# Stage changes of a fused transformer kernel run by token halves

## The reference, cut to what matters

```python
# first block; gate(i), shift(i), scale(i) come from silu(c) @ w_ada + b_ada
h = h + 0.5*gate(0)*rmsnorm(swiglu(modulate(rmsnorm(h, g_pre[0]), shift(0), scale(0))), g_post[0])   # ffn0
p = modulate(rmsnorm(h, g_pre[1]), shift(1), scale(1)) @ w_in      # in_v, in_i, in_t
o = concat([rmsnorm(sparse_attention(p)), rmsnorm(stick_breaking_attention(p))]) @ w_out             # out
h = h + gate(1)*rmsnorm(o, g_post[1])
h = h + 0.5*gate(2)*rmsnorm(swiglu(modulate(rmsnorm(h, g_pre[2]), shift(2), scale(2))), g_post[2])   # ffn1
# second block
h = h + diff_attention(rms_norm(h, attn_norm_g[0])) @ w_o          # v, qk, o_a
h = h + sq_relu_mlp(rms_norm(h, mlp_norm_g[0]))                    # mlp0
h = h + mla_attention(rms_norm(h, attn_norm_g[1]), latents of rms_norm(h, kv_in_norm_g)) @ w_o       # dkv, dq, ..., o_b
h = h + sq_relu_mlp(rms_norm(h, mlp_norm_g[1]))                    # mlp1
return rms_norm(h, final_norm_g)
```

## Time and profile before

| | us |
|---|---|
| median of 3 runs | 1226.72 (1226.50 to 1229.63) |
| the profiled execution | 1227.54 |
| its span, first to last instruction | 1226.2 |
| TensorE busy | 1171.4 (96%) |
| VectorE busy | 796.8 (65%) |
| ScalarE busy | 618.6 (50%) |
| GpSimd busy | 55.8 (5%) |
| mean granted TensorE clock | 0.985 of full speed |

### The profile page before, as it was taken

How to read it: one execution, slowest core, us unless ns; L and a number is a source line. 1 busy time by engine, 2 the same in 40 slices (tenths; PEclk the granted TensorE clock), 3 DMA queues, 4 the chain that set the end, 5 groups by cost and what they waited for, 6 DMA issues and landing times.

```text
span 1226.2 us, 19544 instructions
## 1 busy us (share of the span) xinstructions
PE 1171.4 (96%) x7742; PEld 1074.6 (88%) x7742; DVE 796.8 (65%) x1310; ACT 618.6 (50%) x1114; POOL 55.8 (5%) x75
## 2 busy tenths in 40 slices
PE   4999999999988999999999899999999889999998
PEld 4988799899977999999989788999998778899997
DVE  4879788758654666565667776555557665655554
ACT  5644343646654644444545455554546545555453
POOL 3100000000000000000002110000000100000000
PEclk9999899999998999999999989999999999999999
DMA  8969999443222365654343223545454414554540
GB/s 348 401 261 415 352 344 348 154 180 138 104 98 75 124 240 207 224 218 172 138 176 138 83 104 127 200 175 197 181 190 151 175 35 154 175 200 176 194 150 35
DMA packets 34010, 231.78 MB, mean 189 GB/s; under 512 B 3704, under 2 KB 5120, under 8 KB 6528
## 3 DMA queue, kind: packets, MB, share of 16 engines
q1 hardware_dynamic: 31952, 226.24, 49.9%
q10 hardware_dynamic: 1968, 4.29, 1.0%
HBM read 229.45 MB, written 1.06 MB: 188 GB/s over the span
## 4 chain that ended last, share of the span: by engine, by line
PE 78%; DVE 11%; ACT 5%; issue 2%; DMA 2%; POOL 1%; ACTq 0%; DVEq 0%; SPq 0%; POOLq 0%
PE ps L392 35%; PE pacc L392 34%; DVE wlo L355 3%; PE ps L402 2%; PE ps L405 2%; ACT wk L1020 2%; PE pacc L402 2%; DVE raw L333 1%; DMA raw<-in_stream 1%; ACT whi L354 1%; POOL st L499 1%; PE ps L531 1%; PE pacc L531 1%; DVE st L1015 1%; DVE tmp L668 1%
## 5 line engine op out<-in xcount | busy, mean ns | idle before, releaser
L355 DVE TENSOR_TENSOR wlo<-raw,whi 128x1024 fp32r<-128x1024 f32 x353 | 430.6, 1226 | 194.8 <-ACT whi L354 188.0
L354 ACT ACTIVATE whi<-raw 128x1024 fp32r<-128x1024 f32 x353 | 368.4, 1054 | 164.8 <-PE pacc L392 84.2
L392 PE MATMUL ps<-nhi,whi 128*128 128x256 f32 x1272 | 368.3, 290 | 1.8 <-DVE arena L1270 1.0
L392 PE MATMUL ps<-nlo,whi 128*128 128x256 f32 x1272 | 361.9, 284 | 0.0
L392 PE MATMUL ps<-nhi,wlo 128*128 128x256 f32 x1272 | 361.7, 284 | 0.0
L392 PEld LDWEIGHTS ps<-nhi,whi 128*128 128x128 f32 x1272 | 245.9, 193 | 7.3 <-DVE arena L1270 1.3
L392 PEld LDWEIGHTS ps<-nlo,whi 128*128 128x128 f32 x1272 | 245.9, 193 | 4.9 <-issue 0.8
L392 PEld LDWEIGHTS ps<-nhi,wlo 128*128 128x128 f32 x1272 | 245.7, 193 | 0.0
L743 ACT ACTIVATE sg<-ps 128x256 f32<-128x256 f32 x104 | 39.8, 383 | 164.5 <-PE ps L392 164.3
L392 PE MATMUL pacc<-whi,mhi 128*128 128x512 f32 x240 | 96.5, 402 | 2.4 <-DVE mlo L1192 2.4
L392 PE MATMUL pacc<-wlo,mhi 128*128 128x512 f32 x240 | 94.5, 394 | 0.0
(11 more groups left out here) (305 smaller groups left out, 1784.8 us busy)
## 6 DMA issues: line engine op xcount, KB each, us to landing
raw<-in_stream SPq DMA_DIRECT2D x213, 1024.0 KB, 4.9
gates<-in_g_post ACTq DMA_DIRECT2D x3, 512.0 KB, 6.4
h<-in_x SPq DMA_DIRECT2D x1, 1024.0 KB, 7.0
cst<-in_const ACTq DMA_DIRECT2D x1, 1024.0 KB, 4.8
arena<-bias_rows ACTq DMA_DIRECT2D x1, 1024.0 KB, 18.8
out<-tmp SPq DMA_DIRECT2D x4, 256.0 KB, 2.1
silu_c<-in_c_row ACTq DMA_DIRECT2D x1, 512.0 KB, 5.9
arena<-in_final_g SPq DMA_DIRECT2D x1, 512.0 KB, 5.7
```

Source lines behind the costliest of these rows:

```text
L354: t_hi = act.do(lambda e: e.activation(whi[:, s, :], src, ACT.Copy), arrived, room)
L355: t_lo = dve.do(lambda e: e.tensor_tensor(wlo[:, s, :], src, whi[:, s, :].bitcast(F32), ALU.subtract), arrived, room, t_hi)
L392: return e.matmul(o, lt[a], rh[b], start=start and first, stop=stop and last)
```

## The change

- `last_two` becomes `last_units`: the last three units (`LAST = 3`) run for token half 0, then for half 1. Three hooks of a new class `Crossing` take the place of `residual` and `to_parts`: `first` once half 0 is summed, `between` ahead of half 1's last unit, `second` once half 1 is summed.
- With a gate, y times gate is multiplied before the root of y is known, and the root enters the update of h.
- Turning, scaling and splitting are done for each half by itself, in pairs of chunks: two ScalarE steps of 128 tokens, then one VectorE copy and one subtraction for both chunks. The pieces are interleaved in a written order, with `feed(limit=1)` among them. The second half's turn and parts stand in `finish`.
- The next stage's first four units of `in_v` and `v` run half by half (`lead=cross.finish`: half 0 of two units, `finish`, half 0 of two more, then half 1 of all four); `dkv` and `dq` do likewise. `mlp0`, `mlp1` and `ffn1` begin after `finish`.
- After `mlp1` (`Ending`), h times the final gain is formed before the root, and each half is written by itself.
- `stream_plan`: the eight `ada` units of modulation 7 move from `ffn0` to `in_v`; `IN_ORDER` is another.

```diff
-IN_ORDER = [8, 9, 10, 11] + [g + j for g, j in ((12, 0), (16, 0), (12, 1), (16, 1), (12, 2), (16, 2), (0, 0), (4, 0),
-                                                (12, 3), (16, 3), (0, 1), (4, 1), (0, 2), (4, 2), (0, 3), (4, 3))]
+IN_ORDER = [8, 9, 12, 16, 10, 11, 13, 17, 14, 18, 15, 19, 0, 4, 1, 5, 2, 6, 3, 7]
...
-            if n < j - 1:
+            if n < min(j - 1, blocks - LAST):
                 steps.append(("down", n))
...
-    plan += spread(ffn("ffn0_", DFF // P, ("gate", "up"), 8), (2, 3, 4, 5, 6, 7), 1.03)
-    plan += [("in_v", k) for k in range(8)] + [("in_i", 0)]
+    plan += spread(ffn("ffn0_", DFF // P, ("gate", "up"), 8), (2, 3, 4, 5, 6), 1.05)
+    plan += spread([("in_v", k) for k in range(8)] + [("in_i", 0)], (7,), 1.0)
     plan += [("in_t", j) for j in IN_ORDER]
     plan += [("out", k) for k in OUT_ORDER]
...
-        def feed(until=None):
-            while not hold and pos["unit"] < (until or len(plan)):
+        def feed(until=None, limit=100):
...
+        def last_units(names, meeting, cross, between=None):
+            units, meets, done = [], [], [[None, None], [None, None]]
+            for i in range(2):
+                for n, name in enumerate(names):
+                    if i == 0:
+                        units.append(Unit(name))
+                        meets.append(meeting(n))
+                    meet, late = meets[n]
+                    for f in range(2):
+                        done[i][f] = products([(fix[2 * i + f].ap, [(meet[i], units[n].part(f * 512, f * 512 + 512), late)],
+                                                False, n == len(names) - 1)], units[n].ready)
+                    if i:
+                        units[n].release(done[1][1])
+                        if n == len(names) - 2:
+                            cross.between()
+                    elif between is not None and n < len(names) - 1:
+                        between()
+                if i == 0:
+                    cross.first(done[0])
+            cross.second(done[1])
...
+            if lead is not None:
+                units, start = [], 4
+                for i in range(2):
+                    for n in range(start):
+                        if i == 0:
+                            units.append(Unit(names[n]))
+                        k = chunks[n]
+                        unit_half(n, units[n], i, parts.tokens(k, i), parts.half[k, i])
+                        if i:
+                            units[n].release(done[1][1])
+                            feed()
+                        elif n == 1:
+                            lead()
...
+        class Crossing:
+            def __init__(self, outs, slot=None, gate=None, table=None):
+                self.outs, self.slot, self.gate, self.table = outs, slot, gate, table
+                self.q, self.p, self.r, self.held, self.z = {}, {}, {}, {}, {}
+                self.done, self.diag, self.gated = {}, {}, {}
+            def squares(self, src, n, sums, *after):
+                junk, f = arena[:, 6144 + 512 * n:6656 + 512 * n], n % 2
+                return act.do(lambda e: e.activation(junk, src, ACT.Square, scale=D ** -0.5,
+                                                     accum_out=sums[:, f:f + 1]), *after)
+            def root(self, sums, *after):
+                v, r = new_stat(), new_stat()
+                t = dve.do(lambda e: e.scalar_tensor_tensor(v, sums[:, 0:1], EPS, sums[:, 1:2], ALU.add, ALU.add), *after)
+                return r, power(r, v, t)
+            def begin(self, i, f):
+                w, y, d = slice(f * 512, f * 512 + 512), fix[2 * i + f], self.done[i][f]
+                if f == 0:
+                    self.q[i] = new_stat(2)
+                t = self.squares(y.ap, 2 * i + f, self.q[i], d)
+                tg = dve.do(lambda e: e.tensor_tensor(tmp[:, i, w], y.ap, gates[:, self.slot, w], ALU.mult), t, self.gate())
+                y.free = [tg]
+                self.gated[i, f], self.summed = tg, t
+            def mean(self, i):
+                self.r[i] = self.root(self.q[i], self.summed)
+            def update(self, i, f):
+                w, y = slice(f * 512, f * 512 + 512), fix[2 * i + f]
+                if f == 0:
+                    self.p[i] = new_stat(2)
+                if self.slot is None:
+                    t = dve.do(lambda e: e.tensor_tensor(h[:, i, w], h[:, i, w], y.ap, ALU.add), self.done[i][f])
+                    y.free = [t]
+                else:
+                    r, t_r = self.r[i]
+                    t = dve.do(lambda e: e.scalar_tensor_tensor(h[:, i, w], tmp[:, i, w], r, h[:, i, w], ALU.mult,
+                                                                ALU.add), t_r, self.gated[i, f])
+                self.summed = self.squares(h[:, i, w], 4 + 2 * i + f, self.p[i], t)
+            def ends(self, i):
+                self.r[i] = self.root(self.p[i], self.summed)
+            def diagonal(self, i):
+                r, t = self.r[i]
+                self.diag[i] = diagonal(i, r, t)
+            def turn(self, i):
+                self.held[i] = []
+                for g in range(4):
+                    b = banks.take()
+                    for c in range(2):
+                        k = 2 * g + c
+                        tk = pe.do(lambda e: e.matmul(b.ap[:, c * P:(c + 1) * P], h[:, i, k * P:(k + 1) * P], dg[:, i, :],
+                                                      start=True, stop=True), self.diag[i], b.free)
+                    self.held[i].append((b, tk))
+                dg_free[i] = [tk]
+            def scaled(self, i, *pairs):
+                w = slice(i * P, i * P + P)
+                for g in pairs:
+                    b, tk = self.held[i][g]
+                    for n, (parts, scale, shift, after) in enumerate(self.outs):
+                        for c in range(2):
+                            k, o, z = 2 * g + c, b.ap[:, c * P:(c + 1) * P], self.zs(n)
+                            if shift is None:
+                                t = act.do(lambda e: e.activation(z[:, k, w], o, ACT.Copy, scale=scale(k)), tk, after())
+                            else:
+                                t = act.do(lambda e: e.activation(z[:, k, w], o, ACT.Identity, bias=shift(k),
+                                                                  scale=scale(k)), tk, after())
+                        self.z[n, i, g] = t
+                    banks.give(b, t)
+            def zs(self, n):
+                z = arena[:, 6144:8192] if n else wk[:, 0:6, :].rearrange("p a b -> p (a b)")[:, 0:8 * T]
+                return z.rearrange("p (c t) -> p c t", c=8)
+            def split(self, i, *pairs):
+                for g in pairs:
+                    for n, (parts, scale, shift, after) in enumerate(self.outs):
+                        z = self.zs(n)[:, 2 * g:2 * g + 2, i * P:i * P + P]
+                        hi, lo = (a[:, 2 * g:2 * g + 2, i * P:i * P + P] for a in (parts.hi, parts.lo))
+                        t1 = dve.do(lambda e: e.tensor_copy(hi, z), self.z[n, i, g])
+                        t2 = dve.do(lambda e: e.tensor_tensor(lo, z, hi.bitcast(F32), ALU.subtract), t1)
+                        for k in (2 * g, 2 * g + 1):
+                            parts.half[k, i] = [t1, t2]
+                            if i:
+                                parts.t[k] = parts.half[k, 0] + parts.half[k, 1]
+            def first(self, done):
+                self.done[0] = done
+                if self.slot is None:
+                    self.update(0, 0)
+                    self.update(0, 1)
+                    self.ends(0)
+                    self.diagonal(0)
+                    return
+                self.begin(0, 0)
+                self.begin(0, 1)
+                self.mean(0)
+                if self.table is not None:
+                    act.quiet(self.table)
+                self.update(0, 0)
+                self.update(0, 1)
+            def between(self):
+                if self.slot is None:
+                    self.turn(0)
+                    self.scaled(0, 0, 1)
+            def second(self, done):
+                self.done[1] = done
+                if self.slot is None:
+                    self.update(1, 0)
+                    self.split(0, 0)
+                    self.update(1, 1)
+                    self.scaled(0, 2, 3)
+                    self.split(0, 1)
+                    self.ends(1)
+                    self.split(0, 2)
+                    self.diagonal(1)
+                    self.split(0, 3)
+                    busy(8)
+                else:
+                    self.begin(1, 0)
+                    self.ends(0)
+                    self.begin(1, 1)
+                    self.diagonal(0)
+                    self.mean(1)
+                    busy(20)
+                    self.turn(0)
+                    self.scaled(0, 0, 1)
+                    self.split(0, 0)
+                    self.update(1, 0)
+                    self.update(1, 1)
```

(69 more changed lines are left out.)

235 lines of the change are left out of this document (79 added, 156 removed).

## The result

The changed kernel took 1246.55 us (median of 4 runs, 1245.26 to 1247.86) against 1226.61 for the kernel before beside it: a ratio of 1.0161, 95% interval 1.0135 to 1.0188. It is slower, as forecast, but by 20 us and not by 9.5, and half a microsecond outside the range. The profiled execution's span is 1246.4; the page's first part now reads

The account below looks back on a forecast made before the run. TensorE is busy 96% of the span, so time can only come from pauses, half-speed stretches and instructions without products. 23 + 2 - 0.5 - 1 - 5 - 9 = +9.5 on the median 1226.7 gives 1236 us, range 1219 to 1246.

Parts of the forecast that it names:

- the crossings: The six stage changes, with their waiting, turns and queueing, cost +23 in sum; bounds -2 and +28.
- The clock: PE falls to half speed after a pause, with those in `out` and `v` named: one drop, +2; bounds 0 and 12.
- Rival (3): PE's clock falls in every crossing, at the second turn, after pauses of 1.6 to 4 us: 1242 to 1246; chance 0.16.
- The queues: DVE and ACT issue order at the crossings delays half 1's diagonal and parts; counted within the crossings' +23.
- The lost cover: At `o_a` and `o_b`, half 0's turn no longer covers half 1's chain: +1.8 each if only this counts.
- The root beside the splits: At the crossings, GpSimd's root collides with VectorE splits on the shared SBUF interface: 0.4 at each.
- The plans: Moving modulation 7 out of `ffn0` gives -5; the new `IN_ORDER` gives -9 around `in_t` and `out`.
- The end: After `mlp1`, half 0 is written early and fewer, shorter DVE steps follow the last root: -0.5 (0 to -1).
- The -1 for the waits ahead of the last blocks: Four hidden layers wait 0.26 before their last block; three units now stand ahead: -1.

Follow-up runs that it names:

- fills: Changed kernel with more products of nothing: 44 for 20 ahead of `out`'s second turn, 20 ahead of the third chunk at `ffn1`, `mlp0`, `mlp1`; 1244.75 us.
- mend: Changed kernel without `finish`'s weight unit at `ffn1`, `mlp0`, `mlp1`, lambda load issued ahead of `ffn1`, 44 products of nothing ahead of `out`'s second turn; 1227.81 us.
- mend_turn: `mend` and `turn_behind` together: the three mends and the other order of the no-gate crossings; 1226.32 us (0.9994).
- turn_behind: Changed kernel with, at no-gate crossings, half 0's turn behind half 1's last product, half 1's chain ahead of splits, 4 products of nothing for 20; 1240.25 us.
- lead_turn: `lead_limit` with `turn_behind`'s order at `mlp0` and `mlp1` and no weight unit ahead of their parts; 1233.09 us (1.0044).
- lead_limit: `mend` with no weight or modulation unit issued by the first two units at `in_v`, `v`, `dkv`, the one in `finish` kept; 1236.31 us (1.0068).
- ada_back: Changed kernel with the old `stream_plan`: modulation 7's eight units back in `ffn0`; 1246.5 us.
- parts_first: Changed kernel with `finish`'s weight unit behind half 1's splits and the next stage's first two units kept from issuing any; 1244.67 us (1.0129).
- order_only: Kernel before with the new `IN_ORDER` alone; 1218.72 us (0.9938).

## Why the prediction was wrong

The direction and the mechanisms of the crossings were right; the term for the clock was mis-sized, 2 entered and 10.6 measured, and it makes 8.6 of the miss of 10.7 us (the crossings without the clock are 2.3 over, the rest with the end 1.0, and the plans won 1.2 more than entered). By the forecast's own steps:

- **The clock** failed. "One drop: +2" stood for all six crossings. Five of them dropped, one more than once, and it cost 10.6, inside the bounds of 0 and 12 that I had set for it. I had taken `ffn1`'s and `v`'s pauses of 3.4 and 4 as the ones at risk and set one; the pauses of 2.3 that the same sheet gave for `mlp0`, `mlp1` and `in_v` I priced at their length alone, though the row beside them (2.5 us ahead of 386.65, and 1.8 lost behind it) had their size. Rival (3) had this, with a chance of 0.16 and 1242 to 1246; it placed the drops at the second turn; they came there at `out`, and elsewhere behind the wait for half 1's parts. `fills` shows it at `ffn1` and `mlp0` by taking them away. The Trainium skill's sentence (TensorE: Matmul & The Clock Gate, "Why this matters for your kernels", that idle gaps between bursts send the array back to half clock) speaks of what happened, but the gap's length alone does not tell: in the changed kernel half clock followed all five pauses of 2.46 us and more at the crossings and one of 1.75 at `ffn1`, while `mend` and `fills` had none behind the same pause of 2.46 at `in_v`, nor `mend_turn` behind one of 2.47 at `mlp0`.
- **The queues** were right: 23 forecast, 25.3 measured without the clock; `mlp0` 5.4 and `mlp1` 5.6 against 5.5 and 5.4, `ffn1` 3.7 against 4.1, `v` 4.2 against 4.0. `mend` shows the weight unit and the lambda load as causes. `dkv` was too low (3.9 against 1.9): `Unit` feeds three weight units ahead of half 1's splits there too (3.49 of VectorE from 947.93), which I had counted at `in_v` only. `in_v` was 0.4 too low.
- **The lost cover** was taken with the queueing in one sum of 5.5, of which my lower bound gave it 1.8. In the changed kernel the order is worth 2.4 at each (`turn_behind`, the half clock left out); with the weight unit gone it is 1.0 and 1.2 by `lead_turn` against `lead_limit` (another weight unit included), and less by `mend_turn` against `mend`.
- **The root beside the splits**, entered at 0.4 each, costs nothing: it took 0.55 to 0.60 beside them. The 0.93 stood beside an addition of two SBUF operands of 512 columns; the subtraction of a pair of chunks also reads two, and did not slow it. The Trainium skill's rule of the shared SBUF interface (GPSIMD Engine Reference, "Specifications") is not borne out beside these short steps.
- **The plans** were right: -5 and -9 forecast, -6.1 and -9.1 measured in the changed kernel, -15.1 together by themselves; the pause after `in_t` is gone. What I missed is that the move of modulation 7 and the halves at `in_v` spend the same VectorE time (`ada_back`).
- **The end**: -0.5 forecast, nothing measured: from the start of the last product to the end it is 6.9 in both kernels. Half 0's two output steps stand in VectorE's queue ahead of half 1's updates, which start at 1239.58, as the last product runs, and a gain product of 0.69 stands between the two updates. The -1 for the waits ahead of the last blocks isn't to be seen either.

Left open: why the same wait drops the clock in one execution and not in another, and what remains of 1.4 to 1.5 us at `mlp0` and `mlp1` in `lead_turn` (TensorE waits 1.3 there for the second pair's `nlo`).

## What to carry to other kernels

Splitting a stage change in halves pays only if both queues have room for twice the steps just then: here the old crossings, with both halves' chains under one another, were beaten at one place only (1.0 us at `in_v`, and only with no modulation in VectorE's queue there), and the gain of this change lay in the two plans, which could have been had alone. When a sheet of the queues gives a pause of TensorE, price it as its length plus what the clock does behind it, from the nearest row of the same length, at every place where the sheet has one. Where one wait is taken away, ask who stands next in the same queue: here a modulation, a weight unit and a load each took the place of the other.

## What the runs showed of the hardware that was not expected

- The same wait ahead of the second turn, 1.41 to 1.43 us behind 20 small products, was followed by a turn at full clock in ten cases (2.05) and by a slow one in six (3.35 to 3.68; 3.63 in `parts_first`, 3.68 in `fills`). After the pause of 2.46 at `in_v` in the changed kernel the first products still ran at full clock and the slow ones came from 240.02 on, 1.3 us later. In `turn_behind` the products came out of pauses of 2.47 and 2.46 at full clock; at `mlp0` they fell to half 0.5 us later, at `mlp1` only behind the next pause, of 1.48.
- At `v` in the changed kernel the pause was 6.2 us, and the half clock behind it cost 2.3; behind the pauses of 2.5 at `in_v`, `mlp0` and `mlp1` it cost 1.6, 1.3 and 1.4. The pause counts by its length, the clock behind it by a price of its own that grows little.
- The transfer of the bias table landed 18.8 us after its issue in the kernel before and 24.7 in `order_only`, whose programs are equal up to there; with modulation 7 out of `ffn0` it took 14.5 and 13.9.
